# Gelu of the expert picks as a cubic, a tanh and a halved gate

## The reference

```python
def peer_ffn(x, w_query, sub_keys, down, up):
    H, K, TB = 8, 16, 128                    # heads, picks of a head, tokens of a block
    ...
    top_s, pos = lax.top_k(cand_s, K)        # 16 of 16384 experts, for each token and head
    idx = jnp.take_along_axis(cand_i, pos, axis=-1)
    gate = jax.nn.softmax(top_s, axis=-1)

    def expert_block(args):
        xb, ib, gb = args
        a = jnp.einsum('thkd,td->thk', down[ib], xb)
        c = gb * jax.nn.gelu(a)
        return jnp.einsum('thk,thkd->td', c, up[ib])
```

## Time and profile before

| | us |
|---|---|
| median of 3 runs | 2218.03 |
| lowest and highest of them | 2214.88, 2218.52 |
| the profiled execution | 2219.33 |
| its span, from first to last instruction | 2217.6 |
| outside of the span | 1.7 |

### The profile page before, as it was taken

The page is one execution under the profiler, slowest core; times in us unless marked ns, Lnnn a source line. Parts: engine busy times, 40 slices in busy tenths (PEclk is TensorE's granted clock), DMA queues, the critical chain, the costliest instruction groups (busy, mean ns, idle before and its releaser), DMA issues.

```text
span 2217.6 us, 19179 instructions
## 1 busy us (share of the span) xinstructions
PE 1985.1 (90%) x6132; PEld 1069.0 (48%) x6132; DVE 1292.8 (58%) x3377; ACT 632.7 (29%) x1518; POOL 611.9 (28%) x560
## 2 busy tenths in 40 slices
PE   7999999899999899888889988898989899778777
PEld 5885587588644344443334443443434444223322
DVE  5550264200033568786576877657687757777764
ACT  2000134200024332543142255223235423222221
POOL 1100010000000233343343333334334434444442
PEclk9999999999999999999999999999999999999999
DMA  9998734444676899999999999999999999999997
GB/s 393 420 409 313 262 127 141 169 152 151 237 272 215 319 420 421 421 421 410 421 421 420 421 418 412 405 419 421 419 404 404 416 418 407 422 421 418 421 420 317
DMA packets 110614, 793.89 MB, mean 358 GB/s; under 512 B 12394, under 2 KB 12522, under 8 KB 15674
## 3 DMA queue, kind: packets, MB, share of 16 engines
q0 software_dynamic: 79936, 581.08, 63.6%
q1 hardware_dynamic: 29088, 207.73, 24.9%
q10 hardware_dynamic: 1498, 3.99, 0.5%
HBM read 791.67 MB, written 4.75 MB: 359 GB/s over the span
## 4 chain that ended last, share of the span: by engine, by line
PE 53%; DMA 26%; DVE 11%; ACT 6%; issue 3%; POOL 1%; DVEq 0%; POOLq 0%; ACTq 0%
DMA wide<-experts_in,pick_idx 21%; PE PS L1517 17%; PE PS L1075 15%; PE PS L517 9%; PE PS L1591 6%; DMA ring<-experts_in,pick_idx 4%; DVE wide L1145 3%; PE PS L1797 1%; ACT diag L1061 1%; ACT L1056 1%; DMA early<-ada_in 1%; DVE topi L1093 1%; DVE topi L1096 1%; PE PS L1640 1%; PE PS L511 1%
## 5 line engine op out<-in xcount | busy, mean ns | idle before, releaser
L1075 PE MATMUL PS<-wide,diag 128*128 128x512 f32 x1824 | 880.6, 619 | 167.6 <-ACT diag L1061 160.1
L1220 POOL DMA_INDIRECT wide<-experts_in,pick_idx x456 | 516.4, 1132 | 1179.6 <-PE PS L1075 738.5
L1145 DVE CUSTOM_DVE_ANT_0 wide<-wide,htok 128x1024 f32<-128x1024 f32 x454 | 549.8, 1223 | 216.3 <-DMA wide<-experts_in,pick_idx 206.0
L1075 PEld LDWEIGHTS PS<-wide,diag 128*128 128x128 f32 x1824 | 343.1, 196 | 626.3 <-issue 353.7
L1517 PE MATMUL PS<-hT,ring 128*128 128x256 f32 x1648 | 361.8, 382 | 6.4 <-DMA ring<-wts_in 2.8
L1517 PEld LDWEIGHTS PS<-hT,ring 128*128 128x128 f32 x1648 | 315.2, 192 | 52.6 <-issue 7.3
L517 PE MATMUL PS<-ring,hTm 128*128 128x512 f32 (+1 forms) x704 | 323.3, 588 | 1.9 <-ACT hTm L478 0.8
L1061 ACT ACTIVATE diag<-cst,coef 128x128 f32<-128x128 f32 x510 | 177.0, 394 | 262.1 <-DVE coef L1168 259.1
L1056 ACT ACTIVATE coef<-dots 128x2 f32<-128x2 f32 x255 | 51.9, 204 | 587.6 <-DVE dots L1145 586.8
L517 PEld LDWEIGHTS PS<-ring,hTm 128*128 128x128 f32 x704 | 133.7, 192 | 163.0 <-issue 154.8
L1075 PE MATMUL PS<-ring,diag 128*128 128x512 f32 x224 | 113.0, 628 | 28.0 <-ACT diag L1061 27.9
(11 more groups left out here) (351 smaller groups left out, 1483.2 us busy)
## 6 DMA issues: line engine op xcount, KB each, us to landing
ring<-wts_in SPq DMA_DIRECT2D x191, 1024.0 KB, 4.8
early<-ada_in POOLq DMA_DIRECT2D x36, 1024.0 KB, 12.5
wide<-experts_in,pick_idx POOLq DMA_INDIRECT x456
ring<-wts_in SPq DMA_DIRECT2D x8, 780.0 KB, 4.1
strip_t<-strips_one POOLq DMA_DIRECT2D x1, 2048.0 KB, 20.4
strip_dil<-strips_one POOLq DMA_DIRECT2D x1, 1536.0 KB, 27.6
x<-x_in ACTq DMA_DIRECT2D x1, 1024.0 KB, 5.7
bias_t<-strip_t POOLq DMA_DIRECT2D x1, 1024.0 KB, 9.0
```

Source lines behind the costliest of these rows:

```text
L1075: last = pe.matmul(PS[:, SUMS[i] + half, :], diag[:, n % RING, :], ups(n)[:, half * BANK:(half + 1) * BANK], start=k == 0, stop=k == PICKS ...
L1145: v.tensor_tensor_reduce(out=downs(n), in0=downs(n), in1=htok[:, tb, :], scale=1.0, scalar=0.0, op0=ALU.mult, op1=ALU.add, accum_out=dots[ ...
L1220: pool.indirect_dma_start(row(n), None, experts.rearrange("l e d -> (l e) d"), bass.IndirectOffsetOnAxis(pick_idx[:, u % 4, k:k + 1], 0), ...
```

## The change

Gelu is taken apart. With d the dot, VectorE makes t = 0.044715 d d and y = (t + 1) d (`gelu_in`, two instructions, into the new tile `cube`). ScalarE takes tanh(sqrt(2/pi) y) in place of Gelu. VectorE makes d times the gate (`half_gates`, into the new tile `halves`), and `weigh` now makes (tanh + 1) times that. The factor 0.5 goes into the gates, as a second operation of the instruction at L1138. `dots_done` is raised once a round, by y, where each dot raised it before. VectorE waits for the two dots before t, for t before y, and for `halves`, before it goes on.

```diff
--- before.py
+++ after.py
@@ -7,6 +7,8 @@
 
 
 from contextlib import ExitStack
+
+import math
 
 import numpy as np
 
@@ -51,6 +53,7 @@
 EXPERT_HEADS = 8
 NKEYS = 128
 K16 = 16
+GELU_A, GELU_B = 0.044715, math.sqrt(2.0 / math.pi)
 PICKS = EXPERT_HEADS * K16
 RING = 8
 ROWS = RING + 1
@@ -244,6 +247,8 @@
         pick_idx = sb("pick_idx", [P, 4, K16], U32, stack=two)
         gate = sb("gate", [P, 4, K16], stack=two)
         dots = sb("dots", [P, 2, ROUND], stack=two)
+        cube = sb("cube", [P, 2, 2, ROUND], stack=two)
+        halves = sb("halves", [P, 2, ROUND], stack=two)
         coef = sb("coef", [P, 2, 2, ROUND], stack=two)
         diag = sb("diag", [P, RING, P], stack=two)
 
@@ -1044,16 +1049,16 @@
                     rnd = u * ROUNDS + rr
                     if rnd + 1 == UNITS * LAYERS * ROUNDS:
                         for j in range(ROUND):
-                            act.wait_ge(m["dots_done"], rnd * ROUND + j + 1)
-                            act.activation(coef[:, 0, rr % 2, j:j + 1], dots[:, rr % 2, j:j + 1], ACT.Gelu_apprx_tanh)\
+                            act.wait_ge(m["dots_done"], rnd + j + 1)
+                            act.activation(coef[:, 0, rr % 2, j:j + 1], cube[:, 1, rr % 2, j:j + 1], ACT.Tanh, scale=GELU_B)\
                                 .then_inc(m["gelu_ready"], 1)
                             act.wait_ge(m["coef_ready"], rnd + j + 1)
                             act.wait_ge(m["ups_used"], rnd * ROUND + j + 1 - RING)
                             act.activation(diag[:, (rr * ROUND + j) % RING, :], ident, ACT.Copy, scale=coef[:, 1, rr % 2, j:j + 1])\
                                 .then_inc(m["diag_ready"], 1)
                         break
-                    act.wait_ge(m["dots_done"], rnd * ROUND + ROUND)
-                    act.activation(coef[:, 0, rr % 2, :], dots[:, rr % 2, :], ACT.Gelu_apprx_tanh).then_inc(m["gelu_ready"], 1)
+                    act.wait_ge(m["dots_done"], rnd + 1)
+                    act.activation(coef[:, 0, rr % 2, :], cube[:, 1, rr % 2, :], ACT.Tanh, scale=GELU_B).then_inc(m["gelu_ready"], 1)
                     act.wait_ge(m["coef_ready"], rnd + 1)
                     if rnd * ROUND >= RING:
                         act.wait_ge(m["ups_used"], rnd * ROUND + ROUND - RING)
@@ -1135,28 +1140,43 @@
                     e = topf[:, 128 + 32 * a:144 + 32 * a]
                     V(v.reduce_sum(topf[:, 224:225], e, AX.X))
                     V(v.reciprocal(topf[:, 224:225], topf[:, 224:225]))
-                    V(v.tensor_scalar(gate[:, g % 4, :], e, topf[:, 224:225], None, ALU.mult))
+                    V(v.tensor_scalar(gate[:, g % 4, :], e, topf[:, 224:225], 0.5, ALU.mult, ALU.mult))
+
+            def gelu_in(u, rr, j0, j1):
+
+                d, t, y = dots[:, rr % 2, j0:j1], cube[:, 0, rr % 2, j0:j1], cube[:, 1, rr % 2, j0:j1]
+                V(v.scalar_tensor_tensor(t, d, GELU_A, d, ALU.mult, ALU.mult))
+                v.scalar_tensor_tensor(y, t, 1.0, d, ALU.add, ALU.mult).then_inc(m["dots_done"], 1)
+
+            def half_gates(u, rr, j0, j1):
+                V(v.tensor_tensor(halves[:, rr % 2, j0:j1], dots[:, rr % 2, j0:j1],
+                                  gate[:, u % 4, rr * ROUND + j0:rr * ROUND + j1], ALU.mult))
 
             def dot(u, rr):
 
                 for j in range(ROUND):
                     n = u * K16 + rr * ROUND + j
                     v.wait_ge(rows_loaded[n % ROWS], 16 * (n // ROWS + 1))
-                    v.tensor_tensor_reduce(out=downs(n), in0=downs(n),
-                                           in1=htok[:, tb, :], scale=1.0, scalar=0.0, op0=ALU.mult,
-                                           op1=ALU.add, accum_out=dots[:, rr % 2, j:j + 1]).then_inc(m["dots_done"], 1)
+                    V.go(v.tensor_tensor_reduce(out=downs(n), in0=downs(n),
+                                                in1=htok[:, tb, :], scale=1.0, scalar=0.0, op0=ALU.mult,
+                                                op1=ALU.add, accum_out=dots[:, rr % 2, j:j + 1]))
+                V.done()
+                gelu_in(u, rr, 0, ROUND)
+                half_gates(u, rr, 0, ROUND)
 
             def last_round(u, rr):
                 for j in range(ROUND):
                     n = u * K16 + rr * ROUND + j
                     v.wait_ge(rows_loaded[n % ROWS], 16 * (n // ROWS + 1))
-                    v.tensor_tensor_reduce(out=downs(n), in0=downs(n),
-                                           in1=htok[:, tb, :], scale=1.0, scalar=0.0, op0=ALU.mult,
-                                           op1=ALU.add, accum_out=dots[:, rr % 2, j:j + 1]).then_inc(m["dots_done"], 1)
+                    V(v.tensor_tensor_reduce(out=downs(n), in0=downs(n),
+                                             in1=htok[:, tb, :], scale=1.0, scalar=0.0, op0=ALU.mult,
+                                             op1=ALU.add, accum_out=dots[:, rr % 2, j:j + 1]))
+                    gelu_in(u, rr, j, j + 1)
+                    half_gates(u, rr, j, j + 1)
                     v.wait_ge(m["gelu_ready"], u * ROUNDS + rr + j + 1)
                     v.wait_ge(m["diag_ready"], n - 2)
-                    v.tensor_tensor(coef[:, 1, rr % 2, j:j + 1], coef[:, 0, rr % 2, j:j + 1],
-                                    gate[:, u % 4, rr * ROUND + j:rr * ROUND + j + 1], ALU.mult).then_inc(m["coef_ready"], 1)
+                    v.scalar_tensor_tensor(coef[:, 1, rr % 2, j:j + 1], coef[:, 0, rr % 2, j:j + 1], 1.0,
+                                           halves[:, rr % 2, j:j + 1], ALU.add, ALU.mult).then_inc(m["coef_ready"], 1)
 
             def weigh(u, rr):
 
@@ -1165,7 +1185,7 @@
                 if rnd >= 2:
 
                     v.wait_ge(m["diag_ready"], ROUND * (rnd - 1))
-                v.tensor_tensor(coef[:, 1, rr % 2, :], coef[:, 0, rr % 2, :], gate[:, u % 4, rr * ROUND:(rr + 1) * ROUND], ALU.mult)\
+                v.scalar_tensor_tensor(coef[:, 1, rr % 2, :], coef[:, 0, rr % 2, :], 1.0, halves[:, rr % 2, :], ALU.add, ALU.mult)\
                     .then_inc(m["coef_ready"], 1)
 
             def sum_of(i):
```

## The result

The changed kernel takes 2227.63 us (median of 5 runs, 2226.18 to 2228.93); the kernel before, run beside it, 2217.3 us (5 runs, 2214.88 to 2218.52). The ratio is 1.0045, with a 95% interval of 1.0032 to 1.0058: 10 us slower, between 7 and 13. The profiled execution took 2227.63 us, 8.3 us more than that of before. In the experiments further down, one of the 11 executions of act_all took 5217 us and isn't in its ratio.

A forecast was written before the change was run, and what follows sets the result against it. It took the picks as bound by bytes, at 421 GB/s of DMA. VectorE work not covered in 1619 to 1756 us (2.0 us) plus the end (0.4) gave +2.4 us on 2218.03, so 2220.4; range 2210 to 2229.

The forecast's parts named there:

- the slower rival: VectorE becomes the bound in 1619 to 1756 us, Gelu waits giving back only half: +8.2 us, 2226; chance 0.24.
- the same, +2.4 us: Whole kernel: loads go, the gain ends in VectorE's new work and the byte limit; 2220.4 us, chance 0.46.
- The cost of a round on VectorE: Each of 256 rounds: waits, t, y and `halves` add 0.61 us on VectorE, 156 us in all.
- The loads that stay: ScalarE in the picks: 48 or 54 of 129 table loads stay; 13 or 22 at L1056, 7 or 4 at L1032.
- The waits of `weigh` that the prediction counted: VectorE's waits for Gelu in three stretches, 43.6 us; removed loads give back 10.3, 7.7 and 11.6 us.
- The end: Last pick: nothing covers the longer chain from dot to coefficient, so it ends 0.4 us later.
- the DMA rate from 1619 to 1756 us: Deciding sign: 401 GB/s or so means the forecast, under 395 the slower rival, over 412 the faster.
- the sum by stretches: Per stretch, VectorE's 14.6 us of added work less returned waits, against waiting for rows; 2.0 us over in all.
- It fits: 1240 to 1376 us: 6.9 us of net added work against 9.8 us of waiting for rows, no loss.
- Elsewhere the reserve is larger than what is added: Outside the three stretches VectorE's waiting for rows covers the added work, no loss; from 1890 us, 39 us added.
- It just fits: 860 to 1000 us: 4.3 us of net added work against 4.5 us of waiting for rows, no loss.
- The ring as a reserve of 7.8 us: Queue of gathers in the picks: lateness under about 7.8 us only shortens it; more runs the DMA engines dry.

The follow-up runs named there:

- act_all: Kernel before, with square, tanh, halves and gated coefficient all on ScalarE, VectorE making only the dots, no Gelu loads: 2219.45 us, ratio 1.0000.
- loads_gone: Kernel before with Tanh in place of Gelu on the same dots, no VectorE work added, output not the reference's: 2217.69 us, ratio 0.9998.
- work_double: The double dose: kernel before with the three new VectorE instructions issued twice behind each round's weighing, results unread: 2249.28 us, ratio 1.0133.
- work_behind: Kernel before with the three new VectorE instructions issued once behind each round's weighing, results unread, Gelu and its loads kept: 2226.93 us, ratio 1.0044.
- rows8: Kernel before with eight gather buffers in place of nine: 2218.75 us, ratio 1.0003.
- rows8_change: Changed kernel with eight gather buffers in place of nine: 2229.49 us, ratio 1.0043 against the kernel before.
- rows7: Kernel before with seven gather buffers in place of nine: 2237.34 us, ratio 1.0097.
- work_loads_back: Changed kernel with Gelu in place of Tanh on the cubic, so the table loads return, output not the reference's: 2231.33 us, ratio 1.0055 against the kernel before.
- act_cubic: Kernel before with the cubic, tanh and halves on ScalarE, VectorE's round as before, Gelu's loads gone: 2220.78 us, ratio 1.0009.

## Why the prediction was right or wrong

The range (2210 to 2229) holds the time, and the 28% for "slower" came true, at about the price of the slower rival (2226). But the likeliest case said "the same, +2.4 us", and 10 us were lost. And the slower rival was right in its size only: its mechanism was that the waits for Gelu don't shrink. They did. That the range holds the time is therefore luck: its upper end was priced by a mechanism that didn't happen.

**What held.** The cost of a round on VectorE was 0.61 us by the sum and is 0.58. The loads that stay are 13 and 7, the lower count of the prediction: tanh rides with Exp, with Sigmoid and with Silu. In the trace of the changed kernel the load for a Sigmoid (L353), and elsewhere the one for a Silu (L388), serves the tanh (L1061) behind it too:

```profile
1563.99 1.28 ACT L353 ACT_TABLE_LOAD   x1
1565.28 0.38 ACT L353 ACTIVATE u<-PS 128x256 f32<-128x256 f32 x1
1565.56 0.20 ACT L1061 ACTIVATE coef<-cube 128x2 f32<-128x2 f32 x1
...
923.09 1.28 ACT L388 ACT_TABLE_LOAD   x1
924.38 0.49 ACT L388 ACTIVATE u<-PS 128x384 f32<-128x384 f32 x1
924.77 0.27 ACT L389 ACTIVATE u<-PS 128x128 f32<-128x128 f32 x1
925.05 0.20 ACT L1061 ACTIVATE coef<-cube 128x2 f32<-128x2 f32 x1
```

The Trainium skill ("ScalarE: Activation LUTs", Table sets) lists it with exp and with sigmoid; the trace agrees.

The waits of `weigh` that the prediction counted were to give back 29.6 us. They stood at 15.0, 10.5 and 18.1 us; this is what is left of them in the changed kernel, in the same three stretches:

```profile
DVE coef L1188 <- ACT coef L1061: 1.7, 2, 0.9
DVE coef L1188 <- DVE topi L1101: 1.0, 1, 1.0
...
DVE coef L1188 <- ACT coef L1061: 2.2, 2, 1.6
DVE coef L1188 <- DVE topi L1101: 0.5, 1, 0.5
...
DVE coef L1188 <- issue: 2.2, 1, 2.2
DVE coef L1188 <- ACT coef L1061: 1.6, 2, 0.8
```

That is 9.2 us, so 34.4 were given back, more than the sum had. The end costs 0.4 us too, as said. Its last pick in the changed kernel:

```profile
2217.96 1.22 DVE L1171 CUSTOM_DVE_ANT_0 wide<-wide,htok 128x1024 f32<-128x1024 f32 x1 [0.37 <-DMA wide<-experts_in,pick_idx]
2219.11 0.08 DVE L1171 DVE_READ_ACCUMULATOR2_ANT dots<- 128x1 f32 x1
...
2219.62 0.20 ACT L1053 ACTIVATE coef<-cube 128x1 f32<-128x1 f32 x1 [1.59 <-DVE cube L1149]
```

0.51 us from the read of the accumulator to the tanh, against 0.12 to Gelu: 0.39 us more.

**Its signs.** The one that was to decide, the DMA rate from 1619 to 1756 us, came out at 409 GB/s, which is none of its three answers (401, under 395, over 412). The waits of `weigh` for ScalarE fell to 27.1 us (about 40 was said), the dots' waits for rows to 124.6 (about 100), and ScalarE's busy time fell by 109 us (96 to 104 was said). Neither of the two conditions under which the prediction called itself wrong came true: a round costs 0.58 us, near 0.61, and the shortage doesn't come from ScalarE's loads (loads_gone). None of its signs would have shown the step that failed.

**The step that failed** is the sum by stretches: "It fits" for 1240 to 1376 us, and "Elsewhere the reserve is larger than what is added". Both put the loss at nothing. The shortage grew by 2.6 us in 1240 to 1376 us, and by 6.2 us in 1000 to 1240, 1376 to 1619 and 1756 to 1890 us together. The stretch that the sum counted with 2.0 us has 0.7 less than before. ("It just fits" for 860 to 1000 us held: 421 GB/s, as before.) I set added work against VectorE's waiting for rows, summed over 137 to 313 us, as if a wait late in a stretch could pay for work early in it. VectorE's rounds are very unequal, since the search for the best experts puts up to 3.7 us of instructions into some rounds (1098.29 to 1101.97 us in the kernel before) and none into others. Where such rounds follow each other it was near full already, and the added 0.58 us made it full. That this is what costs the time is argued from the rows, not shown by a run. Busy time by stretches of 10 us, first in the kernel before, then in the changed one, whose picks are 5 us later here, so that the times are the same but not quite the picks:

```profile
1280.00:1290.00 10.00, 8.34 (x29) 4.11 (x28) 8.51 (x23) 4.53 (x10) 4.63 (x4) 1.00 1.01 419
1290.00:1300.00 10.00, 8.18 (x20) 3.25 (x18) 7.78 (x20) 4.99 (x11) 2.92 (x4) 1.00 1.01 411
1300.00:1310.00 10.00, 9.79 (x27) 4.43 (x27) 6.77 (x18) 6.46 (x14) 4.26 (x4) 1.00 1.01 414
```

```profile
1280.00:1290.00 10.00, 7.07 (x12) 2.88 (x13) 9.55 (x27) 4.03 (x10) 2.99 (x3) 0.83 1.01 404
1290.00:1300.00 10.00, 9.63 (x31) 4.70 (x30) 8.67 (x33) 5.41 (x12) 5.01 (x4) 1.00 0.96 334
1300.00:1310.00 10.00, 9.26 (x27) 4.15 (x26) 9.66 (x25) 4.67 (x11) 4.50 (x5) 1.00 0.99 391
```

The third busy number is VectorE's: 8.5, 7.8 and 6.8 us of 10 before, 9.6, 8.7 and 9.7 after, and the DMA rate falls from 419, 411 and 414 to 404, 334 and 391. That alone is 3.2 us of shortage for 0.5. Stretches in which VectorE is busy 9.3 us or more number 3 in the kernel before, 32 in the changed one and 44 with the double dose, with 0.8, 5.7 and 21.9 us of shortage in them. In stretches where TensorE is busy 9.95 us or more the shortage is 5.7 us before and 11.0 after (a stretch can count in both). These are counts, not a proof: loads_gone has 16 full stretches with 4.8 us of shortage and loses no time.

**How 0.58 us become more.** The rows above hold one more number, TensorE's granted clock: 0.83 in the first stretch of the changed kernel, 1.00 before. Here are the same eight matmuls of a round, and the gather that comes after them, before and then after:

```profile
1277.64 1.98 PE L1075 MATMUL PS<-ring,diag 128*128 128x512 f32 x4 [2.75 <-ACT diag L1061]
1279.46 1.88 PE L1075 MATMUL PS<-wide,diag 128*128 128x512 f32 x4
1281.73 0.94 POOL L1220 DMA_INDIRECT wide<-experts_in,pick_idx  x1 [0.31 <-issue]
```

```profile
1282.38 2.51 PE L1080 MATMUL PS<-ring,diag 128*128 128x512 f32 x4 [3.33 <-ACT diag L1066]
1284.69 3.09 PE L1080 MATMUL PS<-wide,diag 128*128 128x512 f32 x4
1288.05 1.73 POOL L1240 DMA_INDIRECT wide<-experts_in,pick_idx  x1 [1.89 <-PE PS L1080]
1284.90:1287.80 2.90, 2.88 (x4) 0.79 (x3) 2.73 (x11) 0.37 (x2) 1.00 (x1) 0.62 1.01 370
1287.80:1292.00 4.20, 3.67 (x9) 1.76 (x10) 4.03 (x13) 0.90 (x3) 2.67 (x2) 1.00 0.88 320
```

VectorE's three instructions make the pause in front of TensorE 0.58 us longer, 3.33 us for 2.75. Behind the longer pause the granted clock is a mix of its two levels, 2.4 and 1.2 GHz (0.62 from 1284.90 to 1287.80), and the eight matmuls take 5.60 us in place of 3.86. The gathers before this round were 4.2 us later than in the kernel before; the one shown is 6.3 us later, and the DMA rate falls to 370 and then 320 GB/s. So 0.58 us of VectorE's work free a buffer 2.2 us later, and the slower matmuls are 1.7 of that. With the double dose the same round pauses 3.67 us, the clock is 0.50 (1.2 GHz) from 1292.30 to 1295.70, and the DMA rate behind it is 196 GB/s.

Only these two places were followed instruction by instruction, and how much of the whole loss goes this way isn't shown. Stretches of 10 us with a granted clock under 0.9, each with the one behind it, hold 4.0 us of the 13.6 of shortage in the kernel before, 8.8 of 21.7 in the changed one, 14.4 of 22.0 in work_behind and 33.8 of 45.2 in work_double. But they also hold 12.9 of 16.6 in loads_gone, which is no slower, and the mean clock from 760 to 2190 us is the same 0.97 before and after. No run changes the clock and leaves VectorE alone.

**The ring as a reserve of 7.8 us** is neither confirmed nor refuted. It told me that lateness of a few microseconds is free, and the single dose isn't free. Between nine and eight buffers neither kernel's time depends on the ring (rows8, rows8_change); with seven it does (rows7). Yet the double dose is near it: 24 rounds of the 0.91 us that it takes in the trace are 21.8 us; less the waits for rows of the prediction (4.5, 9.8 and 1.0 us) and less 7.8 us they leave 9.5, 4.2 and 13.0 us in the three stretches, and heads 2 to 4 of the first three parts lose 11.1, 5.9 and 11.7. That is one trace, and the first of these moves by some 3 us with the limits that one takes.

**The removed loads** were priced well as VectorE's waits (29.6 us; 34.4 came back). In time they are worth nothing without the work (loads_gone, -0.4) and 2 to 4 us with it (work_loads_back), which isn't clear of nothing. So the change paid 10 to 12 us and got at most a few back.

**What stays open.** Why one buffer less leaves both kernels as they are, while VectorE's lateness costs, and how the loss divides between full stretches, TensorE's clock and the mixers' own chain, which VectorE's order delays too. No run here separated these. One way is excluded: that a late search keeps the gathers from being issued. From 760 us on, GpSimd in the changed kernel waits for TensorE (847 us) and never for VectorE's indices.

## What to carry to other kernels

Where an engine's work is uneven, compare added work with its idle time in short stretches (here 10 us; the queue of gathers reached 7.8), not with its idle sum over a stage: VectorE was 58% busy over the span and 72% in the picks, and 9% more of work still cost 0.45%. Look at the granted clock there too: a longer pause in front of TensorE can cost more than its own length. Removed waits on an engine that ends up waiting for the DMA were worth nothing here, so test them alone first, by a kernel that leaves the arithmetic out. If a formula must be rewritten to save table loads, put the extra instructions on the engine that is idle: here all of them fit on ScalarE at no cost, though also at no gain.

## What the runs showed of the hardware

Three instructions of two columns, with the wait for the dots, take 0.58 us, nearly half of a dot product over 1024 columns (1.22). The first block of the network, whose instructions are the same in all kernels, varies from one profile to the next: the first dot started at 752.4 us in the kernel before, at 746.1 in act_cubic and at 752.6 in the changed one. That is 6 us, as much as the effects studied here, so single profiles are best compared from the first dot on: from there to the end of the span the kernel before takes 1465.2 us, the changed one 1473.2, act_cubic 1467.1 and work_double 1496.8. The shortages by fixed stretches, above, don't allow for this.

In one round TensorE's granted clock fell behind a pause of 3.33 us (0.62 from 1284.90 to 1287.80 us in the changed kernel), where behind a pause of 2.75 us it stayed at 1.00 in the kernel before: four matmuls of 512 columns took 3.09 us in place of 1.88.
